# Moving the low weight products of an encoder block's head groups from GpSimd to VectorE

## The reference

```
h = rms_norm(x) * (1 + scale1) + shift1
B, C, u, q, k, v, gA, gB = split(h @ w_in)
y_A = B * dwconv3(C * u)
y_B = windowed_gqa(rms_norm(q), rms_norm(k), v, sink)    # |t-s| <= 128, ALiBi, 16 query heads, 4 key heads
x = x + gate1 * ((sigmoid(gA) * y_A + sigmoid(gB) * y_B) @ w_o)
h = rms_norm(x) * (1 + scale2) + shift2
a, b = split(h @ w_up)
x = x + gate2 * ((gelu(dwconv3(a) + bias) * b) @ w_down)
```

## Time and profile before

| what | value |
|---|---|
| median of 3 runs | 823.35 us (823.16 to 824.01) |
| profiled execution, device time | 821.7 us |
| its span | 819.9 us |
| mean granted TensorE clock | 0.996 |
| VectorE busy | 519.5 us |
| GpSimd busy | 374.3 us |

### The profile page before, as it was taken

The page is one execution under the profiler, slowest core; times in us unless marked ns, Lnnn a source line. Parts: engine busy times, 40 slices in busy tenths (PEclk is TensorE's granted clock), DMA queues, the critical chain, the costliest instruction groups (busy, mean ns, idle before and its releaser), DMA issues.

```text
span 819.9 us, 10342 instructions
## 1 busy us (share of the span) xinstructions
PE 783.2 (96%) x3661; PEld 644.6 (79%) x3661; DVE 519.5 (63%) x722; ACT 374.1 (46%) x664; POOL 374.3 (46%) x221
## 2 busy tenths in 40 slices
PE   4898999999999999999997999999999999999997
PEld 3676787788888888878886888888888888887886
DVE  4748876657765776687438888888888888000000
ACT  6656467556655665455434533434444333112220
POOL 1774523334443443445734345554444455444440
PEclk9999999999999999999999999999999999999999
DMA  9934351333433343434131332223223332223311
GB/s 300 356 119 155 112 182 67 101 131 129 155 100 131 129 155 102 140 118 155 52 103 52 102 100 80 81 98 102 102 102 102 102 102 74 76 91 122 111 52 38
DMA packets 83276, 95.98 MB, mean 117 GB/s; under 512 B 2674, under 2 KB 77610, under 8 KB 83242
## 3 DMA queue, kind: packets, MB, share of 16 engines
q1 hardware_dynamic: 79018, 93.44, 34.2%
q10 hardware_dynamic: 4224, 2.10, 0.9%
HBM read 93.43 MB, written 2.10 MB: 117 GB/s over the span
## 4 chain that ended last, share of the span: by engine, by line
PE 85%; DVE 9%; ACT 3%; issue 1%; DMA 1%; SPq 0%; DVEq 0%
PE bank L794 24%; PE bank L795 24%; PE bank L796 24%; PE bank L926 2%; PE bank L954 2%; PE bank L937 2%; DVE acc L1232 1%; PE bank L842 1%; PE bank L843 1%; DVE pt_lo L1296 1%; DMA ada<-in_w_ada_dram 1%; PE bank L850 1%; DVE a_buf L1320 1%; DVE h_lo L1451 1%; DVE sm L1282 1%
## 5 line engine op out<-in xcount | busy, mean ns | idle before, releaser
L794 PE MATMUL bank<-h_hi,w_hi 128*128 128x512 f32 (+1 forms) x776 | 300.9, 388 | 7.8 <-DVE h_lo L1451 4.3
L795 PE MATMUL bank<-h_lo,w_hi 128*128 128x512 f32 (+1 forms) x776 | 298.4, 384 | 0.0
L796 PE MATMUL bank<-h_hi,w_lo 128*128 128x512 f32 (+1 forms) x776 | 298.3, 384 | 0.0
L420 POOL TENSOR_TENSOR w_lo<-w_raw,w_hi 128x1024 fp32r<-128x1024 f32 x78 | 200.4, 2589 | 205.4 <-ACT w_hi L508 199.7
L427 POOL TENSOR_TENSOR w_lo<-w_raw,w_hi 128x512 fp32r<-128x512 f32 x88 | 124.0, 1431 | 179.8 <-ACT w_hi L508 179.8
L794 PEld LDWEIGHTS bank<-h_hi,w_hi 128*128 128x128 f32 x776 | 146.5, 189 | 37.8 <-DVE h_lo L1451 4.1
L508 ACT ACTIVATE w_hi<-w_raw 128x1024 fp32r<-128x1024 f32 x122 | 124.7, 1052 | 106.6 <-PE bank L796 106.6
L796 PEld LDWEIGHTS bank<-h_hi,w_lo 128*128 128x128 f32 x776 | 146.4, 189 | 29.2
L795 PEld LDWEIGHTS bank<-h_lo,w_hi 128*128 128x128 f32 x776 | 146.5, 189 | 27.4
L794 PE MATMUL bank<-g_hi,w_hi 128*128 128x512 f32 x176 | 70.1, 398 | 0.0
L796 PE MATMUL bank<-g_hi,w_lo 128*128 128x512 f32 x176 | 69.6, 396 | 0.0
(11 more groups left out here) (178 smaller groups left out, 1004.2 us busy)
## 6 DMA issues: line engine op xcount, KB each, us to landing
w_raw<-in_w_in_dram SPq DMA_DIRECT2D x23, 1024.0 KB, 5.2
w_raw<-in_w_up_dram SPq DMA_DIRECT2D x22, 1024.0 KB, 5.1
ada<-in_w_ada_dram SPq DMA_DIRECT2D x32, 512.0 KB, 6.0
ada<-in_w_ada_dram SPq DMA_DIRECT2D x32, 256.0 KB, 7.3
w_raw<-in_w_down_dram SPq DMA_DIRECT2D x8, 1024.0 KB, 5.0
w_raw<-in_w_o_dram SPq DMA_DIRECT2D x4, 1024.0 KB, 5.0
w_raw<-in_w_down_dram SPq DMA_DIRECT2D x4, 768.0 KB, 4.2
x_nat<-in_x_dram SPq DMA_DIRECT2D x4, 512.0 KB, 5.1
```

What stands on the lines that cost most here:

```text
L420: pool.tensor_tensor(w_lo[:, n % 2, u], w_raw[:, n % 2, :, u * P:(u + 1) * P], w_hi[:, n % 2, u], SUB).then_inc(lo_ready, 1)
L794: pe.matmul(dst, w_h, rhs_hi, start=first, stop=False)
L795: pe.matmul(dst, w_h, rhs_lo, start=False, stop=False)
L796: return pe.matmul(dst, w_l, rhs_hi, start=False, stop=last)
```

## The change

The low parts of the units that are prepared during the head groups, pairs 3 to 24, are computed by VectorE, one instruction of 128x1024 for each unit, as the last step of the slot in which ScalarE makes the high copy. The instruction waits for the unit's high copy and for the low part before it. GpSimd keeps in the groups only the slopes, which it scales as soon as the group's last scores are drained, and it waits for the low parts of pair 24 before it goes on with pair 25.

```diff
-            def low_by_halves(n, u):
-
-                pool.wait_ge(hi_ready, 2 * n + u + 1)
-                for k in (slice(0, HT), slice(HT, KT)):
-                    ins = pool.tensor_tensor(w_lo[:, n % 2, u, k, :], w_raw[:, n % 2, k, u * P:(u + 1) * P],
-                                             w_hi[:, n % 2, u, k, :], SUB)
-                ins.then_inc(lo_ready, 1)
-
...
             for g in range(KV):
-                for i in range(2 * len(kinds(g))):
-                    if pair_of(g, i // 2) + 2 <= P_WO:
-                        low_by_halves(pair_of(g, i // 2) + 2, i % 2)
-                    if i == 8 and g < KV - 1:
-                        pool.wait_ge(score_free, (g + 1) * NB * HG + 2)
-                        pool.tensor_scalar(bias[:, :, :], bias[:, :, :], 2.0 ** (-8 * HG // H), 1.0,
-                                           MUL, MUL).then_inc(bias_done, 1)
+                if g < KV - 1:
+                    pool.wait_ge(score_free, (g + 1) * NB * HG + 2)
+                    pool.tensor_scalar(bias[:, :, :], bias[:, :, :], 2.0 ** (-8 * HG // H), 1.0,
+                                       MUL, MUL).then_inc(bias_done, 1)
...
+            pool.wait_ge(lo_ready, 2 * P_WO + 2)
             for n in range(P_WO + 1, P_UP + 1):
                 low(None, 0, n)
...
+                def weights_low(n, u):
+
+                    dve.wait_ge(hi_ready, 2 * n + u + 1)
+                    dve.wait_ge(lo_ready, 2 * n + u)
+                    dve.tensor_tensor(w_lo[:, n % 2, u], w_raw[:, n % 2, :, u * P:(u + 1) * P], w_hi[:, n % 2, u],
+                                      SUB).then_inc(lo_ready, 1)
...
                     if kind and slot // 2 - 1 in GEMV_AT:
                         gemv(g, GEMV_AT[slot // 2 - 1])
+                    if kind and pair_of(g, i) + 2 <= P_WO:
+                        weights_low(pair_of(g, i) + 2, u)
                 dve.wait_ge(o_free, (g + 1) * (2 * NB))
                 merge(0)
                 merge(1)
```

## The result

The changed kernel takes 846.7 us (843.0 to 846.9, 4 runs) against 823.25 (4 runs): a ratio of 1.027, 95% interval 1.025 to 1.030. The forecast was 845.0, from 829 to 862. One execution of the kernel before, run beside three of the experiments, took 3264 us and is left out of every comparison.

What follows compares the result with a forecast made beforehand. TensorE's matmul stream, busy 96% of the span, bounds the kernel; only gaps cost. Group losses 2.7 + 7.4 + 7.4 + 4.2 = 21.7 us on 821.7 give 843.4, plus 1.65 to the median: 845.0, range 829 to 862.

Steps and rivals of the forecast that it cites:

- W: The added VectorE low-part instruction, one per unit of pairs 3 to 24, last in its slot: 44, 56 us in all.
- the sum: Whole kernel: losses of groups 0 to 3, 2.7 + 7.4 + 7.4 + 4.2 = 21.7 us.
- The walk: Slot-by-slot tracing of queue lateness against the old trace, mainly in group 2: 7.4 us there, 2.5 at its head.
- Only the group ends cost: Rival: VectorE's spare time swallows all added instructions but each group's last; 7.5 us lost, 831 us; chance 0.16.
- VectorE as the bound: Rival: each added instruction lies wholly on the path, 56 us, 879 us; half gives 851; chance 0.10 to a large part.
- W's price: Duration of each added VectorE low-part instruction: 1.28 us, bounds 1.27 and 1.38.
- The end of a group: At three group ends the last W delays merges and first drain; TensorE loses 2.5 us each, 7.5 us.
- Inside the groups: Group 2, mid-group: TensorE 3.5 us late at a drain, 4.9 at low parts, 7.8 at a later drain, 8.4 finally.
- the mechanism at slot 12: W there waits for a high copy behind ScalarE's exponentials, holding row factors ScalarE needs; outputs come 7.2 us late.
- Group 0: First head group, no boundary before it: 0.7 at a drain, 0.6 and 0.5 at low parts, 0.9 at outputs: 2.7 us.
- Relief: Rival: silent GpSimd shortens VectorE operations, TensorE's 6.7 us of waits vanish, 817 us; relief or draw 0.08, faster 0.05.
- At nothing: Weights' arrival, loads waiting for them, slopes and GpSimd's wait ahead of the output weights: no cost.

Runs made afterwards that it cites:

- the first experiment: Changed kernel with the last low-part subtraction of groups 0 to 2 moved behind the next group's first score drain: 836.75 us against 821.9, ratio 1.019.
- The late version: Changed kernel with every VectorE low-part subtraction moved one slot later: 822.4 us against 821.9 for the kernel before, ratio 1.000.
- The wait-only runs: Changed kernel, subtraction cut to 128x8, wait kept: 821.2 us, ratio 0.999. Kernel before with only the high-copy waits added to VectorE: 841.7 us, ratio 1.026.
- silence: Changed kernel without the subtraction's work or high-copy wait on VectorE, GpSimd's products also gone: 815.6 us against 821.9 for the kernel before, ratio 0.994.
- the run with waits at the group ends: Kernel before with a VectorE wait for the high copy added only ahead of the merges of groups 0 to 2: 838.9 us against 823.0, ratio 1.019.

## Why the prediction was right, and where its working was not

**Size and sign** held: 845.0 against 846.7. The mechanism is the one forecast: W's wait and place in VectorE's queue hold back what stands behind them. That the numbers meet so closely is in part luck. The trace has four stretches at half clock in the groups, some 6.8 us, for which the sum had no term; without them the groups would have grown by about 19.1 us and not by 25.9, against the 21.7 of the sum. The walk was 2.6 us too high and the clock made up for it.

**The rivals.** Those at 831 and 817 were too low. "Only the group ends cost" fails by the first experiment, too: with the last W of each group out of the way 1.9% is left. VectorE as the bound does not hold: it is busy 65.9 of group 2's 88.5 us. (69 to 70 were forecast; 12 W's came to 14.6 us instead of 15.4, and 5.8 us came back instead of about 3.)

**W's price** was 1.28 us with bounds 1.27 and 1.38; it is 1.22 at the median and 1.227 at most, just under the lower bound. 44 of them are 53.7 us instead of 56.

**The end of a group** was right to the tenth: the merges were expected to start 4.1 us later against TensorE's first scores and came 4.0 later (1.5 us ahead of them before, 2.6 behind them now); a loss of 2.5 us each was expected, and TensorE's second scores come 2.5 us later at this one (2.35 us of it shown as idle time, the same at all three), 7 us for the three together in the first experiment.

**Inside the groups** the walk had TensorE 3.5 us late behind the drain ahead of the earlier trace rows's first line, 4.9 behind the low parts, 7.8 behind slot 15's drain and 8.4 at the end. Of the kernel before, have the scores at 273.86 and 291.51; the product with the third tile's low part was:

```profile
281.53 0.39 PE L954 MATMUL bank<-pt_lo,v_st 128*64 128x512 f32 x1
```
The same three in the changed kernel:

```profile
290.26 1.12 PE L916 MATMUL bank<-k_st,q_st 128*128 128x384 f32 x4 [0.18 <-DVE prob L1265]
298.85 0.44 PE L944 MATMUL bank<-pt_lo,v_st 128*64 128x512 f32 x1 [0.23 <-DVE pt_lo L1286]
311.28 0.86 PE L916 MATMUL bank<-k_st,q_st 128*128 128x256 f32 x4 [2.19 <-DVE prob L1265]
```

With 13.25 us taken off for the group's later start (250.69 - 237.44), TensorE is 3.15, 4.1 and 6.5 us late, and no later at the end. So the steps were in the right places and each a little too large, the last one not there at all. The largest, 2.4 us, is the mechanism at slot 12, seen here in group 1 as W waiting for the copy behind the exponentials, with the row factors after it; moving that W alone took the wait from 2.2 to 0.5 us.

```profile
213.39 1.22 DVE L1308 TENSOR_TENSOR w_lo<-w_raw,w_hi 128x1024 fp32r<-128x1024 f32 x1 [1.23 <-ACT w_hi L498]
214.54 0.15 DVE L1280 TENSOR_TENSOR sm<-sm 128x4 f32<-128x4 f32 x1
214.73 0.18 DVE L1281 RECIPROCAL sm<-sm 128x4 f32<-128x4 f32 x1
218.40 0.87 DVE L1295 TENSOR_TENSOR y_buf<-bank,y_buf 64x256 f32<-64x256 f32 x2 [3.50 <-ACT y_buf L645]
219.30 0.69 DVE L1328 SCALAR_TENSOR_TENSOR a_buf<-b_buf,a_buf 128x512 f32<-128x512 f32 x1
219.91 1.28 DVE L1222 SCALAR_TENSOR_TENSOR acc<-ada,c_act,acc 128x1024 f32<-128x1024 f32 x1
221.10 1.22 DVE L1308 TENSOR_TENSOR w_lo<-w_raw,w_hi 128x1024 fp32r<-128x1024 f32 x1
222.24 0.87 DVE L1265 SCALAR_TENSOR_TENSOR prob<-bank,sm,bias 128x256 f32<-128x256 f32 x2
```

The outputs at 218.40 wait 3.50 us for ScalarE, which waited for the row factors of 214.73. I had the total for group 2 at 7.4 us; it is 6.6.

**Group 0** was mis-sized: 2.7 expected, 6.8 measured. TensorE's waits there grew by 2.0 us (the drain's 2.00 became 2.13, the outputs' 0.98 became 2.20, one low part's is 0.43, the keys' 1.48 became 1.66). The rest is three stretches at half clock, some 5 us, where the kernel before has none between 64 and 155 us. The sum had no term for what a stall does to the clock, and the prediction's list of waits had left out the one for the keys.

**The weakest part** is not a step of the walk but what it took for the cost. It added up W's length, and its wait at slot 12 and at the group's end, and nothing in it tells which of the two matters. In group 2's trace the W's of slots 6, 8, 10 and 14 wait for nothing, as the walk had it; those of slots 2 and 4 wait 2.37 and 2.57 us, and of all 44 there are 21 that wait, 36.1 us together. The late version shows that the same length costs nothing against the kernel before where the wait isn't. The wait-only runs show the wait at 0.5% above silence, and at 2.6% above the kernel before where GpSimd's product starts on the same signal.

**Relief** was real and small: GpSimd's silence takes 0.6% off, 5 us, against the 6.7 us forecast as its limit. In the run with waits at the group ends two-input merges beside GpSimd's products take 1.66 and 1.75 us instead of 0.69. The Trainium skill ("SBUF — State Buffer", "Who interferes with whom") states that a VectorE instruction with two SBUF inputs contends with a GpSimd instruction that reads SBUF. There the trace agrees that one holds up the other; it doesn't show by what port.

**At nothing:** right. In the head groups no list of waits has TensorE or ScalarE waiting for a transfer or a low part of weights.

## What to carry to other kernels

Before work is moved to the end of another engine's turn, ask what it waits for there, and not only how long it takes: an in-order queue passes a wait on to all that stands behind it. If the product isn't needed soon, put the instruction one turn later, where its input has long arrived; that alone turned a loss of 2.7% into none here. Be wary of releasing two engines by the same signal when both then read SBUF: here that made three waits without work cost 1.9%. And look at TensorE's granted clock behind each new wait, since a stretch at half clock can cost nearly as much as the wait itself.

## What the runs showed of the hardware

In the head groups TensorE's granted clock fell to half, mostly for about 3.4 us, behind some waits of 2.0 to 4.3 us and not behind others of the same length (2.35 us at 166.7 and not at 256.5 in one trace). The changed kernel's mean was 0.982 in three of its executions and 0.986 in the fourth, which was 3.7 us faster with the same program. What decides it was not tested.

A VectorE operation with two inputs in SBUF and 1024 columns takes 1.22 us as a plain subtraction and 1.28 as multiply-and-add with a scalar per partition.
